# A macaron encoder kernel: each mixer begins with four value blocks, and its output projection is regrouped at the end

## The reference

```python
for i in range(DEPTH):
    h = swiglu(x, ffn_w_gate[i, 0], ffn_w_up[i, 0], ffn_w_down[i, 0])
    x = layer_norm(ALPHA * x + 0.5 * h, ln_g[i, 0], ln_b[i, 0])
    ...
    if i % N_MIXERS == 0:
        y = chunked_rel_attention(x, w_qkv_a[j], w_o_a[j], rel_bias)
    else:
        y = stick_breaking_attention(x, w_qkv_b[j], w_o_b[j])
    x = layer_norm(ALPHA * x + y, ln_g[i, 1], ln_b[i, 1])
    h = swiglu(x, ffn_w_gate[i, 1], ffn_w_up[i, 1], ffn_w_down[i, 1])
    x = layer_norm(ALPHA * x + 0.5 * h, ln_g[i, 2], ln_b[i, 2])
```

## Time and profile before

| | |
|---|---|
| median of 3 runs | 1007.55 us (1006.53 to 1008.38) |
| profiled execution | 1008.05 us, span 1006.1 us |
| busy TensorE | 986.4 us, 98% of the span |
| busy VectorE, ScalarE, GpSimd | 572.4, 444.3, 43.8 us |
| mean granted TensorE clock | 0.991 |

### The profile page before, as it was taken

The page is one execution under the profiler, slowest core; times in us unless marked ns, Lnnn a source line. Parts: engine busy times, 40 slices in busy tenths (PEclk is TensorE's granted clock), DMA queues, the critical chain, the costliest instruction groups (busy, mean ns, idle before and its releaser), DMA issues.

```text
span 1006.1 us, 13252 instructions
## 1 busy us (share of the span) xinstructions
PE 986.4 (98%) x5158; PEld 831.0 (83%) x5158; DVE 572.4 (57%) x624; ACT 444.3 (44%) x507; POOL 43.8 (4%) x72
## 2 busy tenths in 40 slices
PE   8999999989999999999999999998999999999997
PEld 6888888889987888888888888887999878888885
DVE  5555463746666645554664555448566685545634
ACT  5443452247663444443344443443465444344430
POOL 1100000001101000000000000001111110000000
PEclk9999999989999999999999999999999999999999
DMA  9965546446552765557556565654444526664521
GB/s 318 286 190 187 206 179 219 147 154 209 195 159 75 233 202 168 182 193 251 168 173 203 167 190 187 250 168 138 155 173 164 167 102 209 192 198 176 208 84 42
DMA packets 136951, 182.80 MB, mean 182 GB/s; under 512 B 5936, under 2 KB 120784, under 8 KB 136912
## 3 DMA queue, kind: packets, MB, share of 16 engines
q1 hardware_dynamic: 134032, 173.56, 52.1%
q0 software_dynamic: 2592, 8.17, 2.5%
q10 hardware_dynamic: 288, 0.52, 0.2%
HBM read 181.16 MB, written 1.07 MB: 181 GB/s over the span
## 4 chain that ended last, share of the span: by engine, by line
PE 94%; DVE 3%; issue 1%; DMA 0%; POOL 0%; ACT 0%; POOLq 0%; SPq 0%
PE psum L368 30%; PE psum L370 29%; PE psum L369 29%; PE psum L405 2%; PE psum L531 1%; PE psum L541 1%; PE psum L552 1%; PE psum L356 1%; DVE stats L842 1%; DVE x L862 1%; DVE x L838 1%; DMA raw<-in_ffn_w_up 0%; DVE xT_lo L825 0%; DVE w_lo L795 0%; POOL rstd L1005 0%
## 5 line engine op out<-in xcount | busy, mean ns | idle before, releaser
L795 DVE TENSOR_TENSOR w_lo<-raw,w_hi 128x2048 fp32r<-128x2048 f32 x162 | 368.8, 2287 | 151.2 <-ACT w_hi L618 150.9
L618 ACT ACTIVATE w_hi<-raw 128x2048 fp32r<-128x2048 f32 x162 | 303.2, 1908 | 93.8 <-PE psum L370 92.1
L368 PE MATMUL psum<-w_hi,xT_hi 128*128 128x512 f32 (+1 forms) x832 | 316.6, 380 | 1.4 <-DVE w_lo L804 1.4
L370 PE MATMUL psum<-w_hi,xT_lo 128*128 128x512 f32 (+1 forms) x832 | 310.9, 374 | 0.0
L369 PE MATMUL psum<-w_lo,xT_hi 128*128 128x512 f32 (+1 forms) x832 | 310.4, 373 | 0.0
L368 PEld LDWEIGHTS psum<-w_hi,xT_hi 128*128 128x128 f32 x832 | 156.7, 188 | 30.1 <-DVE w_lo L804 2.4
L370 PEld LDWEIGHTS psum<-w_hi,xT_lo 128*128 128x128 f32 x832 | 156.6, 188 | 28.3
L369 PEld LDWEIGHTS psum<-w_lo,xT_hi 128*128 128x128 f32 x832 | 156.9, 189 | 25.9
L368 PE MATMUL psum<-w_hi,hT_hi 128*128 128x512 f32 x416 | 163.7, 394 | 0.0
L370 PE MATMUL psum<-w_hi,hT_lo 128*128 128x512 f32 x416 | 162.0, 390 | 0.0
L369 PE MATMUL psum<-w_lo,hT_hi 128*128 128x512 f32 x416 | 162.0, 389 | 0.0
(11 more groups left out here) (71 smaller groups left out, 509.3 us busy)
## 6 DMA issues: line engine op xcount, KB each, us to landing
raw<-in_ffn_w_down SPq DMA_DIRECT2D x88, 512.0 KB, 4.1
raw<-in_ffn_w_gate SPq DMA_DIRECT2D x86, 512.0 KB, 4.0
raw<-in_ffn_w_up SPq DMA_DIRECT2D x86, 512.0 KB, 4.9
raw<-in_w_qkv_a SPq DMA_DIRECT2D x24, 512.0 KB, 4.7
raw<-in_w_qkv_b SPq DMA_DIRECT2D x24, 512.0 KB, 4.6
raw<-in_w_o_a SPq DMA_DIRECT2D x8, 512.0 KB, 3.8
raw<-in_w_o_b SPq DMA_DIRECT2D x8, 512.0 KB, 4.0
gain<-in_ln_g POOLq DMA_DIRECT2D x6, 512.0 KB, 4.0
```

Source lines behind the costliest of these rows:

```text
L368: pe.matmul(acc, st[0], mv[0], start=first, stop=False)
L370: return pe.matmul(acc, st[1], mv[0], start=False, stop=last)
L618: act.activation(w_hi[slot][:], raw[raw_slot][:], ACT.Copy).then_inc(hi_done, 1)
L795: dve.tensor_tensor(w_lo[slot][:], raw[raw_slot][:], w_hi[slot][:], ALU.subtract).then_inc(lo_done, 1)
```

## The change

The tables of blocks are rewritten. `FIRST_BLOCKS` has six blocks in place of four: all four blocks of v0 and v1 come first, then q and k of pair 0. So each later block of q, k and v moves forward by about two places, and half blocks of o fill the last three pairs (1, 3 and 5 of them, where it was 0, 2 and 6 in pairs 5, 6 and 7). The split of unit 4 (the q of group 1) moves ahead of pair 0 on both engines, the units in `AHEAD` move forward with the blocks, and `MIX_SLOTS` has another rotation of buffers. At the end, `head_out(7)` is followed by the half blocks of group 3 on row half 0, split by key block: first the part that needs only pair 6 for both column halves, then the part that needs pair 7. What is computed is the same.

```diff
-FIRST_BLOCKS = [("v", 0, 0), ("v", 1, 0), ("q", 0, 0), ("k", 0, 0)]
-DURING = [[("v", 0, 1), ("q", 0, 1), ("k", 0, 1)],
-          [("v", 1, 1), ("q", 1, 0), ("k", 1, 0)],
...
-          [("k", 3, 0), ("q", 3, 1), ("v", 3, 0)],
-          [("k", 3, 1), ("v", 3, 1), ("o", 0, 0, 0), ("o", 1, 0, 0)],
-          [("o", 0, 0, 1), ("o", 0, 1, 0), ("o", 0, 1, 1), ("o", 1, 0, 1), ("o", 1, 1, 0), ("o", 1, 1, 1)]]
-LAST_TURNED = [("o", 2, 0, 0)]
-LAST_OUT = [("o", 2, 0, 1), ("o", 3, 0, 0), ("o", 3, 0, 1), ("o", 2, 1, 0), ("o", 2, 1, 1), ("o", 3, 1, 0)]
+FIRST_BLOCKS = [("v", 0, 0), ("v", 1, 0), ("v", 0, 1), ("v", 1, 1), ("q", 0, 0), ("k", 0, 0)]
+DURING = [[("q", 0, 1), ("k", 0, 1), ("q", 1, 0)],
+          [("k", 1, 0), ("q", 1, 1), ("k", 1, 1)],
...
+          [("k", 3, 1), ("v", 3, 0), ("o", 0, 0, 0)],
+          [("v", 3, 1), ("o", 1, 0, 0), ("o", 0, 0, 1), ("o", 1, 0, 1)],
+          [("o", 0, 1, 0), ("o", 1, 1, 0), ("o", 0, 1, 1), ("o", 1, 1, 1), ("o", 2, 0, 0)]]
+LAST_TURNED = [("o", 2, 0, 1)]
+LAST_OUT = [("o", 3, 0, 0), ("o", 3, 0, 1), ("o", 2, 1, 0), ("o", 2, 1, 1), ("o", 3, 1, 0)]
...
-AHEAD = [(None, 5), (6, 7), (8, 9), (10, 11), (12, None), (13, 14), (15, 16), (17, None)]
+AHEAD = [(5, 6), (7, 8), (9, None), (10, 11), (12, 13), (14, 15), (16, None), (17, None)]
...
             def out_half(m, g, r, half, kks=(0, 1)):
...
-                if (g, r, half) == (0, 0, 1):
+                if (g, r) == (0, 0) and half == 1:
+
+                    pe.wait_ge(proj_copied, (m + 1) * len(BLOCKS) - 1)
+                if (g, r, half) == (0, 1, 0):
                     pe.wait_ge(proj_copied, (m + 1) * len(BLOCKS))
...
-                proj_block(m, 3)
+                for i in range(3, len(FIRST_BLOCKS)):
+                    proj_block(m, i)
                 scores(m, 0)
...
                 head_out(m, PAIRS - 1)
+                for half in range(2):
+                    out_half(m, GROUPS - 1, 0, half, kks=(0,))
                 for todo in LAST_OUT:
-                    out_half(m, *todo[1:])
+                    out_half(m, *todo[1:], kks=(1,) if todo[1:3] == (GROUPS - 1, 0) else (0, 1))
...
                 copy_proj(m, 2)
                 copy_proj(m, 3)
+                hi_unit(n0 + 4)
+                copy_proj(m, 4)
+                copy_proj(m, 5)
                 weights(m, 0)
-                hi_unit(n0 + 4)
...
-                for n in range(n0 + 2, n0 + 4):
+                for n in range(n0 + 2, n0 + 5):
                     lo_unit(n)
```

More of the change, by code:

```diff
@@ L96 @@
 FFN_SLOTS = [j % 4 for j in range(24)] + [4, 0, 1, 2, 3, 0, 4, 2, 3]
-MIX_SLOTS = [0, 1, 4, 2, 3] + [4, 0, 1, 2, 3] * 2 + [4]
+MIX_SLOTS = [0, 1, 4, 2, 3, 0, 4, 1, 2, 3, 4, 0, 1, 2, 3, 4]
 SLOT = (FFN_SLOTS + MIX_SLOTS + FFN_SLOTS) * DEPTH
@@ L415, in chunk_in_loop, with half_block @@
                 gate_up(1, par, slot, n, True).then_inc(unit_used, 1)
-            def half_block(r, half, d, n, count, ready=None, y=Y):
+            def half_block(r, half, d, n, count, ready=None, y=Y, kks=(0, 1)):
                 s = SLOT[n]
                 rows, cols = slice(r * P, (r + 1) * P), slice(half * HALF, (half + 1) * HALF)
-                for kk in range(2):
+                for kk in kks:
                     k = 2 * d + kk
@@ L500, in proj_block, with out_half @@
                 last.then_inc(proj_done if b == 0 else unit_used, 1)
-            def out_half(m, g, r, half):
+            def out_half(m, g, r, half, kks=(0, 1)):
                 n = MIX_UNIT[m] + 3 * GROUPS + g
@@ L514, in out_half @@
                 last = half_block(r, half, g, n, GROUPS,
-                                  lambda kk: pe.wait_ge(headout_lo, m * PAIRS + 2 * g + kk + 1), Y_MIX)
+                                  lambda kk: pe.wait_ge(headout_lo, m * PAIRS + 2 * g + kk + 1), Y_MIX, kks)
+                if kks == (0,):
+                    return
                 if (r, half) == (1, 1):
@@ L964, in mixer_vector @@
                         break_sticks(m, pp)
-                    if pp == 0:
-                        lo_unit(n0 + 4)
                     during, before = AHEAD[pp]
```

## The result

The changed kernel takes 997.15 us as the median of 5 executions (996.89 to 997.54). The kernel before takes 1008.1 us on the same chip (5 executions, 1006.53 to 1008.38). The ratio is 0.9895, with a 95% interval of 0.988 to 0.9909: about 1% faster. The forecast was 996.2 us.

What follows compares the result with a forecast made beforehand. TensorE, 94% of the span, was taken as the bound. Two mixers, each gaining 6.4 us at the front and losing 0.7 at the end, give 11.4 us: 1007.55 to 996.2 us, range 994.5 to 1000.5.

Steps and rivals of the forecast that it cites:

- Front: Mixer start, transposes to scores: four value blocks first remove the 3.6 us stall and 2.7 us of half clock; gain 6.4.
- small wait for the last piece of `xT_lo`: In the first value block behind a mixer's transposes: this wait and the restart were counted as 0.2 us.
- Moved waits: Mixer start: splits of q0 and k0 and copies of v are ready when TensorE reaches the q and k blocks; no cost.
- Pairs: Pairs 5 to 7: shorter covers of 7.1, 7.0 and 6.8 us still outlast the probabilities' 6.1 us; cost 0.
- Rival B: Short pairs wait in mixer 1 or a split is late, costing 1 to 3 us: about 998.3 us, chance 0.12.
- End: Mixer end: first y comes 0.68 us later in TensorE's work, the wait grows from 0.38 to 1.06; loss 0.7 us.
- the one that hung the restart on the first sum alone: Mixer end: TensorE's restart at the x of row half 1 is at a fixed distance behind the first y.
- about 2.1 us in total for x: Sign in the changed profile: TensorE's wait of L356 for x sums to about 2.1 us in place of 0.8.
- Rival A: Mixer end: the 1.06 us wait brings a spell of half clock, 2.7 us each: 1001.6 us, chance 0.07.
- The rule on short idle times: Skill's report that short idle times between matmul groups made the clock swing; applied to the mixer end's grown 1.06 us wait.
- C: Mixer start: the stall only moves to the third block, gaining 0.2 us a mixer: 1008.6 us, chance 0.03.
- D: Pairs 5 to 7: grown waits each bring half clock, 14.1 us a mixer; in mixer 1 alone 1010.3 us, chance 0.04.

Runs made afterwards that it cites:

- e4: Kernel before with 27 matmuls, their result thrown away, filling the stall ahead of q0 in each mixer: 1003.45 us, ratio 0.9961.
- e3: Changed kernel with the fourth value block moved from the front back into pair 0: 998.4 us, ratio 0.9913.
- e7: Changed kernel with the split of q1 (unit 4) back behind the work on the first scores: 999.52 us, ratio 0.9923.
- e1: Changed kernel with the old end of a mixer put back and the remainder of unit 17 behind pair 6's head output on VectorE: 995.96 us, ratio 0.9886.

## Why the prediction came out right

- **Front, 6.4 us a mixer:** it measured 6.27 in mixer 0 (13.34 + 5.76 - 12.83) and 6.36 in mixer 1. In mixer 0, the small wait for the last piece of `xT_lo` and its restart were taken as 0.2 us. They were 0.14 us beyond a step and 0.11 in the step behind it, and the first step behind the transposes was 0.08 us slow, which I had not counted. Both halves of the term were tested: e4 gives the clock its own price, e3 shows the idle time shrinking with the blocks.
- **Moved waits hold at nothing:** right. e7 shows that it was not free by itself: without the earlier split of q1, 1.8 us of waits come.
- **Pairs at nothing:** right. The rows of mixer 1, pair 6, show TensorE's scores, GpSimd's mask, VectorE's product and TensorE's transposes:

```profile
769.63 0.93 PE L536 MATMUL psum<-kT,qT 64*128 64x128 f32 x8
...
771.56 1.73 POOL L1061 TENSOR_SCALAR_AFFINE_SELECT stick<-stick 128x512 f32<-128x512 f32 x1 [7.31 <-ACT stick L717]
...
775.66 0.96 DVE L949 TENSOR_TENSOR probs<-probs,stick 128x766 f32<-128x766 f32 x1
...
777.57 0.60 PE L546 MATMUL psum<-ident,probs 128*128 128x128 f32 x4
```

From 775.66 + 0.96 = 776.62 to 777.57 there is 0.95 us of slack; the prediction said 0.9. Rival B did not come, and e1 shows that even 5.4 us of cover in pair 7 are enough.

- **End, a loss of 0.7 us a mixer:** the direction was right, the size was 0.56 (e1: 0.6). The step that was off is the one that hung the restart on the first sum alone, at a fixed 12.17 us behind it. In the kernel before it hung on the other chain, and the first had at most 0.13 us to spare (12.17 - 12.04). Of the 0.56 us, 0.34 are the longer wait at the x of row half 1 and 0.22 a slower start of the transposes of row half 0, which the list of waits does not count; the sign "about 2.1 us in total for x" took all of it as listed, and 1.4 are. What the restart hung on shows in the last piece of row half 0, the high part on ScalarE and the remainder on VectorE, before and then in the changed kernel:

```profile
317.16 0.60 ACT L654 ACTIVATE xT_hi<-psum 128x512 fp32r<-128x512 f32 x1 [1.39 <-PE psum L356]
317.80 0.69 DVE L825 TENSOR_TENSOR xT_lo<-psum,xT_hi 128x512 fp32r<-128x512 f32 x1
...
311.43 0.60 ACT L662 ACTIVATE xT_hi<-psum 128x512 fp32r<-128x512 f32 x1 [1.44 <-PE psum L356]
312.42 0.67 DVE L835 TENSOR_TENSOR xT_lo<-psum,xT_hi 128x512 fp32r<-128x512 f32 x1
```

Before, the remainder began 0.04 us behind the end of the high part (317.76), so it was taken as soon as it could be; in the changed kernel it began 0.39 us behind it (312.03), as VectorE, later by then, was still busy.

- **Rival A, a fall of the clock at the grown wait:** it did not come. The waits there are 0.72 us at the x of row half 1 and 0.2 us within the transposes of row half 0 (0.82 us in place of 0.60); the profiled execution has a mean clock of 0.999, and the windows of e3 stay at 1.00 behind 0.51 us. The window of the changed kernel behind its wait of 0.72 us:

```profile
316.00:318.00 2.00, 1.78 (x10) 1.00 0.04 8
```

The trace of the kernel before already had a wait between the 0.38 and the 3.6 us that the prediction compared, at the kernel's start and so not in dense work: 1.2 us for the first weights, in the list of waits and in the window around it.

```profile
PE psum L368 <- DVE w_lo L804: 1.4, 2, 1.2
...
5.00:10.00 5.00, 3.44 (x18) 1.00 1.07 364
```

The rule on short idle times of the Trainium skill, "TensorE: Matmul & The Clock Gate", section "A second HAM failure mode: psum-queue depth-cycling", which stood against the change in the prediction, is not borne out by this kernel's waits. They are few, while the page's kernel idles frequently between groups of matmuls; that case no run here tests.

- **C and D:** excluded by the list of waits.

The forecast was 0.95 us too low. In the profiled executions the gain is 1008.05 - 996.91 = 11.1 us against 11.4. The two mixers gave the 11.4 (5.67 and 5.76), partly by luck, as the front gave a little less than forecast and the end cost a little less; the missing 0.3 us lie ahead of mixer 0, where the prediction had no term. The other 0.7 us lie in the step to the median: I set the median of the changed kernel 0.5 us below its profiled execution, as it was before, and it is 0.24 us above. An offset between one execution and the median is scatter, and the changed kernel has little of it.

## What to carry to other kernels

When the densest engine stalls, look at the granted clock behind the stall and price both: its own length and the slow stretch, if there is one. Here a stall of 3.6 us had one, worth 2.1 to 2.7 us, and waits of 0.72 us and less had none. Work that needs only what is already there belongs in such a place. The split of the unit that comes next had to move too (e7).

Before an end is regrouped to free an engine earlier, ask from which event the restart hangs. Here moving work ahead of the last head output left less of it to cover the norm, and the old end was better by 1.1 to 1.2 us; making the first sum still earlier gained nothing, as a second chain of nearly the same length stood behind it.

## What the runs showed that I had not expected

The half clock behind a stall of 3.6 us is not the same in each execution. In the round of e1 to e4, the kernel before took 1004.25 us in one execution, with a mean clock of 0.997, and 1008.45 us in another, with 0.991. The changed kernel, without the stall, stays within 1.04 us over its nine executions (996.63 to 997.67). e4, which only fills the stall, stays within 0.84 us over six (1002.88 to 1003.72). So taking out the stall also took out most of the scatter, and the gain measured depends on which execution of before is compared.
